# One ring for loaded weight blocks and their remainders, four more pages, and three shifts in the order of side work

## The reference

```python
def second_block(x, positions, ...):
    for l in range(DEPTH_2):                                   # two layers
        h = rms_norm(x, ln_mix_pre[l])
        proj = h @ w_in[l]
        c_q, c_kv, k_pe, conv_u, r_q, r_k, r_v, r_g, gate_logits = jnp.split(proj, points, axis=-1)
        y_mla = mla_branch(...)         # 8 heads of attention over all 512 keys
        y_conv = conv_branch(conv_u, conv_w_dw[l], ...)   # gated, 31 taps per channel (512 channels), layer norm, silu, 512 -> 1024
        y_ret = retention_branch(...)   # 4 heads, each 2 x 128 value channels, group norm over 256, gate, 1024 -> 1024
        gates = jax.nn.sigmoid(gate_logits).reshape(B, S, N_BRANCH, D_MODEL)
        merged = gates[:, :, 0] * y_mla + gates[:, :, 1] * y_conv + gates[:, :, 2] * y_ret
        x = x + rms_norm(merged @ w_out[l], ln_mix_post[l])
        h = rms_norm(x, ln_ffn_pre[l])
        f = (jax.nn.silu(h @ ffn_w_gate[l]) * (h @ ffn_w_up[l])) @ ffn_w_down[l]
        x = x + rms_norm(f, ln_ffn_post[l])
    return x
```

## Time and profile before

| | |
|---|---|
| median of 3 runs | 2884.16 us |
| the profiled execution | 2885.52 us, its span 2883.6 us |
| PE busy | 2810.5 us (97%) |
| DVE, ACT, POOL busy | 1286.2, 1132.0, 1194.7 us |
| layer 0 of the second block, mixing part | about 920 to 1510 us |
| layer 1 of the second block, mixing part | about 1915 to 2503 us |

### The profile page before, as it was taken

The page is one execution under the profiler, slowest core; times in us unless marked ns, Lnnn a source line. Parts: engine busy times, 40 slices in busy tenths (PEclk is TensorE's granted clock), DMA queues, the critical chain, the costliest instruction groups (busy, mean ns, idle before and its releaser), DMA issues.

```text
span 2883.6 us, 34400 instructions
## 1 busy us (share of the span) xinstructions
PE 2810.5 (97%) x13706; PEld 2244.0 (78%) x13706; DVE 1286.2 (45%) x1712; ACT 1132.0 (39%) x1685; POOL 1194.7 (41%) x539
## 2 busy tenths in 40 slices
PE   7999999999999999999999999999999999999999
PEld 6777778888888776787788888867757868788887
DVE  4776424611113867836315202277677353341123
ACT  4334643432233555433334322245544233443222
POOL 2123234354443662453444444436625434344442
PEclk9999999999999999999999999999999999999999
DMA  7343223232223211222232222232102213232222
GB/s 257 118 147 137 75 81 110 105 112 101 95 95 126 81 66 31 73 95 74 90 121 85 99 95 95 99 103 79 66 30 80 96 66 106 97 105 95 95 95 80
DMA packets 89278, 277.97 MB, mean 96 GB/s; under 512 B 9952, under 2 KB 10272, under 8 KB 89120
## 3 DMA queue, kind: packets, MB, share of 16 engines
q1 hardware_dynamic: 89120, 275.78, 27.9%
HBM read 268.40 MB, written 7.34 MB: 96 GB/s over the span
## 4 chain that ended last, share of the span: by engine, by line
PE 87%; DVE 9%; ACT 2%; issue 1%; DMA 0%; SPq 0%; DVEq 0%; ACTq 0%
PE bank L1690 23%; PE bank L1692 23%; PE bank L1691 23%; PE bank L2014 2%; PE bank L1823 2%; PE bank L1966 1%; PE bank L1739 1%; PE bank L1740 1%; PE bank L1741 1%; PE bank L1716 1%; PE bank L1708 1%; PE bank L1709 1%; DVE pageF L2823 1%; PE bank L1978 1%; DVE pageF L2373 1%
## 5 line engine op out<-in xcount | busy, mean ns | idle before, releaser
L2972 POOL TENSOR_TENSOR wlo<-wraw,whi 128x1024 fp32r<-128x1024 f32 x429 | 1044.4, 2437 | 1472.7 <-ACT whi L2043 1458.3
L1690 PE MATMUL bank<-pageR,whi 128*128 128x512 f32 x3184 | 1285.9, 404 | 6.4 <-ACT pageF L2296 1.6
L1692 PE MATMUL bank<-pageR,wlo 128*128 128x512 f32 x3184 | 1230.9, 387 | 0.0
L1691 PE MATMUL bank<-pageR,whi 128*128 128x512 f32 x3184 | 1229.7, 386 | 0.0
L1690 PEld LDWEIGHTS bank<-pageR,whi 128*128 128x128 f32 x3184 | 599.5, 188 | 159.0 <-issue 40.0
L1691 PEld LDWEIGHTS bank<-pageR,whi 128*128 128x128 f32 x3184 | 599.9, 188 | 135.8 <-issue 22.8
L1692 PEld LDWEIGHTS bank<-pageR,wlo 128*128 128x128 f32 x3184 | 599.0, 188 | 123.6
L2043 ACT ACTIVATE whi<-wraw 128x1024 fp32r<-128x1024 f32 x429 | 450.6, 1053 | 414.4 <-PE bank L1692 323.0
L2117 ACT ACTIVATE pageR<-pageF 128x512 fp32r<-128x512 f32 x136 | 86.0, 632 | 425.8 <-DVE pageF L2682 189.0
L2823 DVE SCALAR_TENSOR_TENSOR pageF<-pageF,prm 128x497 f32<-128x497 f32 (+9 forms) x180 | 191.5, 1064 | 2.5
L2981 POOL TENSOR_TENSOR pageR<-pageF,pageR 128x512 fp32r<-128x512 f32 x46 | 66.7, 1462 | 145.7 <-ACT pageR L2117 109.9
(11 more groups left out here) (237 smaller groups left out, 2601.0 us busy)
## 6 DMA issues: line engine op xcount, KB each, us to landing
wraw<-in_wst SPq DMA_DIRECT2D x429, 512.0 KB, 3.5
pageF<-in_wmod SPq DMA_DIRECT2D x96, 256.0 KB, 4.7
pageF<-in_xT SPq DMA_DIRECT2D x16, 256.0 KB, 4.0
pageF<-in_bias SPq DMA_DIRECT2D x16, 256.0 KB, 3.8
kept<-pageF SPq DMA_DIRECT2D x16, 256.0 KB, 5.2
pageF<-kept SPq DMA_DIRECT2D x16, 256.0 KB, 4.1
out_x<-pageF SPq DMA_DIRECT2D x8, 256.0 KB, 2.0
pageF<-in_cT SPq DMA_DIRECT2D x4, 256.0 KB, 10.1
```

Source lines behind the costliest of these rows:

```text
L1690: e.matmul(o, hi, xh, start=first, stop=False)
L1691: e.matmul(o, hi, xl, start=False, stop=False)
L1692: i = e.matmul(o, lo, xh, start=False, stop=last)
L2972: e.tensor_tensor(wlo[:, b % NH, :, :], wraw[:, b % NR, :, :], bc(whi[:, b % NH, :, :]), ALU.subtract).then_inc(*wlod.up(("wlo", b)))
```

## The change

- `wraw` and `wlo` become one ring of six (`NL`) in one place: POOL writes the remainder over the loaded block. The load of block b waits for PE to have finished block b − 6. In the list, the load of block b + 2 follows the split of block b (b + 3 before). POOL no longer waits for `wdone` itself. The two rings of 3 and 4 were 28 KB in each partition, the ring of six is 24 KB; with the rest of the free SBUF the number of pages grows from 70 to 74.
- `mm_turned` cuts its matmuls at the ends of both rings.
- The taps of channel tile 2 stand one to a step.
- Convolution: four yields in place of two between squares and their product. Retention: three in place of two.
- `main_branch`: the gate loop and the wait in the plan look at the first six inputs only; with eight inputs (branch 2), output tile 0 waits in the plan for each input as it comes to it.

```diff
-NR, NH = 3, 4
-NPAGE = 70
+NL, NH = 6, 4
+NPAGE = 74
@@ w_split(self, b)
-            self.w_load(b + NR)
+            self.w_load(b + (3 if b < 3 else 2))
@@ taps(m)
-                if n % 3 or m == 3:
+                if m == 3 or m < 2 and n % 3:
                     yield
@@ side_conv_norm()
-            yield
-            yield
+            yield from pause(4)
             r = yield from sq.rstd_steps(512, "ones", sbk)
@@ side_ret()
-                yield
-                yield
+                yield from pause(3)
                 r = yield from sq.rstd_steps(256, "ones", sbk)
@@ main_branch(i, key, n, w)
-            while (not all(x in made for x in xs) or ahead < 3) and ahead < 4 and len(pages.free) >= 8:
+            early = xs[:6]
+            while (not all(x in made for x in early) or ahead < 3) and ahead < 4 and len(pages.free) >= 8:
...
-            yield from p.ready(*xs)
+            yield from p.ready(*early)
...
-                yield from proj(w + L, m, xs)
+                if m == 0 and n > 6:
+                    yield from p.free_banks(mb, 1)
+                    o = mb.take(("o", w + L, 0))
+                    for k, x in enumerate(xs):
+                        yield from p.ready(x)
+                        step("mm", p.w_next((w + L, 0, k)), ((o, x),), k == 0, k == n - 1)
+                        if k % 2:
+                            yield
+                else:
+                    yield from proj(w + L, m, xs)
@@ program()
-        wraw = sb("wraw", [128, NR, 8, 128])
+        with nc.sbuf_tensor("wraw", [128, NL, 8, 128], F32) as wraw:
+            pass
+        wlo = sb("wlo", [128, NL, 8, 128], F32R)
         whi = sb("whi", [128, NH, 8, 128], F32R)
-        wlo = sb("wlo", [128, NH, 8, 128], F32R)
@@ sync: w_load(b)
-                if b >= NR:
-                    w.wait_ge(*when("whi", b - NR))
-                    w.wait_ge(*when("wlo", b - NR))
+                if b >= NL:
+                    w.wait_ge(*when("wdone", b - NL))
@@ gpsimd: w_split(b)
-                if b >= NH:
-                    w.wait_ge(*when("wdone", b - NH))
@@ tensor: mm_turned
-                    for c, d in ((0, min(n, ring - a)), (ring - a, n)):
...
+                    for c, d in zip(cuts, cuts[1:]):
```

More of the change, by code:

```diff
@@ L1492, in program @@
         wlod, low = (Signal(sem(n), at) for n in ("s_wlo", "s_pool"))
-        raw = [Signal(sem(f"s_raw{i}"), at) for i in range(NR)]
+        raw = [Signal(sem(f"s_raw{i}"), at) for i in range(NL)]
         land = [Signal(sem(f"s_land{i}"), at) for i in range(NLAND)]
@@ L1593, in w_load @@
             def w_load(b):
[L1594 to L1597 removed]
+                if b >= NL:
+                    w.wait_ge(*when("wdone", b - NL))
+                e.dma_start(wraw[:, b % NL, :, :], a["wst"][b]).then_inc(*landed(raw[b % NL], "wraw", b))
             def load_fixed(name):
@@ L1679, in mm @@
                 b, j = divmod(s, 8)
-                hi, lo = whi[:, b % NH, j, :], wlo[:, b % NH, j, :]
+                hi, lo = whi[:, b % NH, j, :], wlo[:, b % NL, j, :]
                 w.wait_ge(*when("whi", b))
@@ L1708, in mm_first_part @@
                     e.matmul(bank(name), whi[:, b % NH, j, :], xh, start=first, stop=False)
-                    e.matmul(bank(name), wlo[:, b % NH, j, :], xh, start=False, stop=False)
+                    e.matmul(bank(name), wlo[:, b % NL, j, :], xh, start=False, stop=False)
             def mm_second_part(slots, outs, x, last):
@@ L1723, in mm_turned @@
             def mm_turned(s, n, outs, x, first, last, final):
-                a, ring = s % (8 * NH), 8 * NH
                 hi, lo = (y[:, :, :, :].rearrange("p b j f -> p (b j) f") for y in (whi, wlo))
+                cuts = sorted({0, n, *(c for ring in (8 * NH, 8 * NL) for c in [ring - s % ring] if c < n)})
                 for b in range(s // 8, (s + n - 1) // 8 + 1):
@@ L1734, in mm_turned @@
                     xh, xl = (half(x, part)[:, 128 * t:128 * t + 128] for part in ("hi", "lo"))
-                    for c, d in ((0, min(n, ring - a)), (ring - a, n)):
[L1736 to L1741, removed]
+                    for c, d in zip(cuts, cuts[1:]):
+                        o, h0, l0 = bank(name)[:, 128 * c:128 * d], (s + c) % (8 * NH), (s + c) % (8 * NL)
+                        h, r = hi[:, h0:h0 + d - c, :], lo[:, l0:l0 + d - c, :]
+                        e.matmul(o, xh, h, start=first and c == 0, stop=False, skip_group_check=True)
+                        e.matmul(o, xl, h, start=False, stop=False, skip_group_check=True)
+                        i = e.matmul(o, xh, r, start=False, stop=last and d == n, skip_group_check=True)
                     names = [name] if last else []
@@ L2042, in w_split @@
                     w.wait_ge(*when("wdone", b - NH))
-                e.activation(whi[:, b % NH, :, :], wraw[:, b % NR, :, :], ACT.Copy).then_inc(*whid.up(("whi", b)))
+                e.activation(whi[:, b % NH, :, :], wraw[:, b % NL, :, :], ACT.Copy).then_inc(*whid.up(("whi", b)))
             def square(t, i, src, c0, width, need, scale):
@@ L2967, in w_split @@
             def w_split(b):
-                if b >= NH:
-                    w.wait_ge(*when("wdone", b - NH))
                 w.wait_ge(*when("wraw", b))
                 w.wait_ge(*when("whi", b))
-                e.tensor_tensor(wlo[:, b % NH, :, :], wraw[:, b % NR, :, :], bc(whi[:, b % NH, :, :]),
+                e.tensor_tensor(wlo[:, b % NL, :, :], wraw[:, b % NL, :, :], bc(whi[:, b % NH, :, :]),
                                 ALU.subtract).then_inc(*wlod.up(("wlo", b)))
```

## The result

The changed kernel takes **2907.9 us** in the median of four runs (2907.5 to 2909.4), beside 2884.8 for the kernel before (2880.9 to 2889.2): ratio 1.0084, interval 1.0072 to 1.0096. It is 23 us slower; 2887.0 was forecast, with a range up to 2900. The profiled execution has a span of 2907.6 us, 24.0 more than before.

The account below looks back on a forecast made before the run. PE was taken as the bound, busy 2810.5 of 2883.6 us. Terms −2.1 − 0.8 + 2.5 + 1.8 = +1.4 a layer, +2.8 in two, gave 2887.0 us; own range 2879 to 2895, with rivals 2865 to 2900.

Parts of the forecast that it names:

- Ring and loads: Block loads now waiting for PE to finish block b − 6: no wait added or removed, 0, upper end 2 us.
- One more yield in retention: At retention's square_sum, a step more covers the waits of heads 0 and 2: −2.1 us a layer, bounds 0 and −2.1.
- Head 3 and the early branch: Head 3's wait of 1.30 goes, but w_ro slots 6 and 7 are one step nearer: −0.8 us a layer, at worst +0.1.
- Four pages: Gate 0 is made earlier, so w_mo slot 3 waits for the last heads' attention output: +2.5 us a layer, bounds 0 and 5.
- Attention stretch: Gate 0 fills the bare stretch's first four steps; the later waits on ACT's exponentials stay: 0, bounds −3.2 and 0.
- Taps of tile 2 and two more yields: Convolution's mean waits 1.85 for 0.83, its norm 3.05 for 2.25: +1.8 us a layer, bounds −4.7 and +5.
- Rival B: DVE becomes the bound in retention's heads 0 and 1, at the value products: +6.4 us a layer, 2897; chance 0.20.
- Rival A: New yields cover the convolution's and retention's waits, DVE being free at the taps' end: −8 us a layer, 2868; chance 0.33.

Follow-up runs that it names:

- experiment 3: The kernel before with only the one ring of six blocks and the 74 pages, taps, sums and branch as before: 2889.9 us, 1.0018.
- experiment 2: The kernel before with only the later sums: four yields for two at the convolution's norm, three for two in every retention head: 2884.4 us, 0.9997.
- experiment 6: The changed kernel with the old 70 pages, so no gate tile is made ahead of the middle branch in the bare attention stretch: 2900.4 us, 1.0053.
- Experiment 1: The kernel before with only the third channel tile's convolution taps set one to a step: 2910.7 us, 1.0089.
- Experiment 9: The changed kernel with the third tile's taps 1 to 30 in layer 0 on 64 of 512 columns, layer 1 as control: 2901.7 us, 1.0058.
- experiment 13: The changed kernel with five yields ahead of the products for the convolution's mean and eight ahead of its norm's: 2886.5 us, 1.0008.
- 14: Experiment 8's kernel with three yields for two in retention's head 0 too: 2878.7 us, 0.998.
- experiment 8: The kernel before with three yields ahead of the convolution's mean, four ahead of its norm, three for two in retention's head 2 alone: 2872.4 us, 0.9957.

## Why the prediction was wrong

The direction of the central case held (slower), and its size didn't: +2.8 forecast, +23 found. By its own steps, a layer:

- *Ring and loads, 0*: as far as shown, right. ACT waits for no block's load in the changed kernel or in experiment 3; no run has the ring alone.
- *One more yield in retention, −2.1*: the waits of heads 0 and 2 went as forecast. But experiment 2 shows that head 0's is only moved, to head 1's products (1.1), which the forecast had held at nothing. Its bound of 0 was the better value for head 0; head 2's 0.79 was real.
- *Head 3 and the early branch, −0.8*: found +0.1. The wait of 1.30 and the 0.3 went, 1.57 + 0.16 = 1.73 came at `w_ro`: the "at worst" end. The early branch is no edit at all.
- *Four pages, +2.5*: found 2.09 + 0.16 = 2.25, at `w_mo` slot 3 and behind POOL, as worked out. Experiment 3 adds what was not seen: without the dense taps the same step costs as much at `w_pw`. Nor was it seen that beside the dense taps the four steps also put a gate's tanh ahead of the norm's squares: the old 70 pages give back 7.5 us in two layers (experiment 6), more than this term.
- *Attention stretch, 0*: right to 0.5, a wait of that size ahead of it.
- ***Taps of tile 2 and two more yields, +1.8*: this step failed.** Found +10.7: head 1's products 2.05 (forecast 0), the mean 3.77 for 1.85, the norm 5.24 for 3.05, the lower clock 4.3 for 1.6. Against the earlier trace rows that is 2.05 + 2.94 + 2.99 + 2.7, twice the upper bound of +5. Experiment 1 shows this edit to cost the whole loss by itself.

These five make −2.1 + 0.1 + 2.25 + 0.5 + 10.7 = 11.5 a layer, 23 in two.

What was wrong in the failed step? First, DVE was taken as in time at head 1's start. It wasn't: with one tap in each step, one split and one of POOL's remainders in its way, its decayed scores came 1.9 late. Experiment 9 shows that the taps' load makes this and 1.4 of the mean's wait. Second, only DVE was followed, and ACT taken as free. Ahead of the mean, ACT did a gate's tanh and a table load before the exponential, so the `rstd` instructions ended 8.8 us after the product and not 6.8: this is about the 1.9 by which the mean's 3.77 exceeds the 1.85 (the tanh itself had waited for DVE, so part of it is the taps' load). Between the mean and the norm, ACT was held by head 1's last output, then by a table load (1.28), a tanh and a rounding, all ahead of the squares: 13.1 us from the mean's product to the last add, where the forecast had 8.1 to 9.9. Experiment 9 keeps the norm's wait at 5.1 without the taps' load, so it is order, not load; experiment 13 brings it to 1.1 by spacing, and experiment 6, where the tanh and its table load stand elsewhere, to 1.8. Third, a second spell at the lower clock was in the bounds and not in the value; it came.

Rival B named the right place (value products, waits at line 2014 over 1 us) and a cost of 6.4 a layer; 11.5 was found. Its condition, DVE over 2 us behind at head 1's scores, was about met (1.9). It had a chance of 0.20. Rival A's argument, DVE busy only 36 of 54 us, was no evidence: at the places where PE needed it, DVE was behind ACT and POOL.

What stays open: of the norm's 13.1 us, no run separates what ACT's queue costs from what the second split costs, as experiment 6 changes both. And the shares of the edits don't add up (+25, +4.6 and −1 us alone, +23 together), so a share given to a step above is what was found at its place, not what undoing it would give.

## What to carry to other kernels

Price a moved step by the chain that it joins, across all engines' queues: what stands ahead of it on ACT and POOL decides, not the busy share of the engine that it uses. A wait can be covered for good only where its own consumer has slack: count the steps from its last output to the first use (eight here; three of them, with one more yield at head 2, gave 12 to 14 us), else it comes back at the next product, as in experiments 2 and 14. And a page, a yield or a tap moved by a step shifts which operations meet POOL's splits, 2 us each, so judge such edits by several placements.

## What the runs showed of the hardware

A spell at half clock does not follow from the wait ahead of it alone. In the kernel before, PE waits 0.80 us at 532.57, and in experiment 8's kernel 0.80 at 532.12, for the same instruction. The stretches behind, first of before, then of experiment 8's kernel (columns as in the earlier trace rows):

```profile
533.18:536.60 3.42, 3.42 (x11) 2.33 (x12) 0.49 (x3) 0.47 (x2) 0.00 (x0) 0.50 0.06 23
```

```profile
533.18:536.60 3.42, 3.13 (x13) 1.70 (x14) 1.46 (x5) 0.66 (x3) 0.00 (x0) 1.00 0.03 7
```

The one has the spell, 1.7 us, the other none. A few such spells, in places that no edit touched, make differences of 2 to 5 us between traces (experiments 8 and 14), as large as the waits that such edits are about. The kernel before itself took from 2879.8 to 2889.2 us over its runs, so one trace of a kernel gives its waits better than its time.

Of a DVE operation and a split, the one that starts first goes first here. The adds that started inside a split ended 0.56 us after it (1208.33 after 1207.77), while a split that began 0.65 us before a running sum ended took 2.88 us in place of 2.40, and the sum its usual 0.69.
